# The weight sums of a block product, kept in DRAM, and a ring of nine operand slots in a one-core hybrid decoder layer

## The chip, the cores and the metric

One core of one Trainium2 chip runs the whole layer. The metric is the device time of one execution in microseconds (us). Five engines work side by side and meet at semaphores: TensorE (PE), VectorE (DVE), ScalarE (ACT), GpSimd (POOL) and SyncE (SP). SP issues the plain transfers, and POOL issues those that add to their destination, besides the stores. In the trace they form two queues, q1 (hardware_dynamic, SP) and q0 (software_dynamic, POOL), which share the core's 16 DMA engines.

## What is computed

The layer takes x (512 tokens by 2048) and gives x plus a merge of two token mixers (reference, cut):

```
h = rms_norm(x, norm_w)
proj = h @ w_in                       # q|k|v|z of both branches, beta, alpha, gates
oa = gated_delta_rule(...)  -> rms_norm -> * silu(gdn_z)      # 8 heads of 128
ob = moba_attention(...)             -> * silu(moba_z)        # 8 heads of 128
y_gdn  = oa @ w_out_gdn               # (512 x 1024) @ (1024 x 2048)
y_moba = ob @ w_out_moba              # (512 x 1024) @ (1024 x 2048)
merged = sigmoid(g_gdn) * y_gdn + sigmoid(g_moba) * y_moba
x = x + merged @ w_o                  # (512 x 2048) @ (2048 x 2048)
```

## The kernel before

**Heads.** The first 920 us or so work on the 8 heads. Each head takes eight stripes of w_in (1 MB each, tile `w_raw`, ring of four), and PE's windows of 48 matmuls on a stripe alternate with the small matmuls of the head. Every float32 product is made of three matmuls of rounded parts: ACT writes the high part (`split`, L1328), and DVE the low part (L1784). SP loads stripe n when window n-4 has ended, and ACT splits it when window n-2 has ended. In the last head DVE also makes sums of blocks of h, in 20 steps (`own_step`, L2271, tile `sg`), which POOL stores to DRAM (`store_own`, L757, `row_sums<-sg`). Step (6, 1), the sixth sum of the second half, waits until the store (1, 1) has landed, because it overwrites the tile. SP loads the sums back for the first quad.

**Quads.** Then come ten quads of 1024 output columns: q = 0 to 3 the gates, 4 and 5 y_gdn, 6 and 7 y_moba (Y0 = 4, YB = 6), 8 and 9 the output projection (W0 = 8). Each quad is a 2 by 2 block product made with seven products in place of eight, in the order P11, PS1, PS2, P12, PS4, PS3, P22. Three of the right operands are blocks of the weights as they are (11, 21, 22), and four are sums of blocks: T1 for PS1, T2 for PS2, T3 for PS3, T4 for P22. A product is cut into units of 256 rows by 512 columns of weights (512 KB), four units in quads 0 to 3, 8 and 9 and two in quads 4 to 7. There are 224 units. For unit n ACT writes the high part (`op_hi`, L1627), DVE the low part (`op_lo`, L2285), and PE runs 12 matmuls (L1268, L1270, L1272). ACT may start unit n when PE has ended unit n-4.

**How the sums come about before.** SP loads the blocks into 12 slots of `ops` (A, B, C with four each). DVE forms T1 (`form_t1`, L2386), T2 of the quads with two units (`form_t2`, L2395), T4 (`form_t4`, L2405) and T3 of the gate quads (`form_t3`, L2413) in place, one instruction of 128 x 1024 each. POOL adds a block to a slot by an accumulating DMA (`add_22`, L771; `add_12`, L777). A later load into a slot waits until the sums that read it are formed. DVE's program is a list written out by hand: `forms(q, n)` puts the forming instructions between the `op_lo`.

**Ends of products.** When a product ends, DVE adds its banks to a block (`block_add`, L2305, L2307). In quads 4 to 7 it then multiplies the block by a gate block (L2316), which SP loads (L615, `operands<-gates`) into one of two tiles. In quads 4 and 5 POOL stores the block (`branch_a`, L788). In quads 6 and 7 POOL adds that stored block to it (L794, `e_block<-branch_a`), PE transposes it (`merged_turn`, L1286, four units after the product), ACT copies it, and DVE and ACT make the left operands of quads 8 and 9 (`merged_step` L2258, `merged_hi` L1715, `merged_lo` L2321).

**POOL in a head,** in program order: `decay_parts` (L707 to L718), the load of decay rows (L702), the store of the previous head's attention output (L733, `branch_outputs<-probs`), the cosine products of k and q (L747), the store of o (L749). After the last head come the last store of probs (L766) and the four `add_22` of quad 0. ACT's rounding of the third block sum of quad 0 (L1701) waits for that store of probs, since it writes where probs lay.

## Time and profile before

| what | us |
|---|---|
| median of 3 runs (1563.8 to 1564.4) | 1563.98 |
| the profiled execution | 1563.22 |
| its span, first to last instruction | 1561.6 |
| PE busy in the span | 1532.2 |
| DVE busy | 1108.2 |
| ACT busy | 766.5 |
| POOL busy | 199.0 |

The profiled execution spent 1.6 us outside the span, and it was 0.8 us shorter than the median. PE's clock was granted in full in all of the 40 slices. Idle time of an engine that is not waited for costs nothing, so the reader looks first at where PE stands still, and then at what it stands still for.

### The profile page before, as it was taken

What the parts mean: (1) busy time and instruction counts of PE and PEld (TensorE: products, weight loads), DVE (VectorE), ACT (ScalarE), POOL (GpSimd) and SP (SyncE); (2) the same over time, 40 slices, a digit from 0 to 9 for tenths busy, and PEclk for the clock granted to TensorE, in tenths of its full rate; (3) what the DMA queues carried; (4) which work ended last, traced back from release to release, by engine and by line L of the source; (5) the groups of instructions that cost most, each with busy time, mean ns of one, the idle gap of its engine ahead of it and who ended that gap; (6) DMA issues with size and microseconds to landing.
All of it is one profiled execution on the core that took longest, in us unless ns stands there. A gap on an engine that the chain in (4) does not pass through costs nothing. (4 is left out here: it accounts for less than half of the span.)

```text
span 1561.6 us, 20373 instructions
## 1 busy us (share of the span) xinstructions
PE 1532.2 (98%) x7591; PEld 1280.8 (82%) x7591; DVE 1108.2 (71%) x1371; ACT 766.5 (49%) x1007; POOL 199.0 (13%) x181
## 2 busy tenths in 40 slices
PE   6999999999999999999999999999999999998999
PEld 5888888888888888888888887888888877876787
DVE  6665756756757656557668869867777999878864
ACT  6434435345435345344344347647465865555542
POOL 4202002002002011011020101001010111102020
PEclk9999999999999999999999999999999999999999
DMA  8314315133324233233144357586567688978883
GB/s 274 82 42 128 82 44 145 54 87 102 80 64 124 60 83 98 60 98 111 34 114 108 115 197 207 191 224 215 146 188 196 216 256 242 243 215 167 225 186 56
DMA packets 198047, 217.02 MB, mean 139 GB/s; under 512 B 7843, under 2 KB 140198, under 8 KB 196902
## 3 DMA queue, kind: packets, MB, share of 16 engines
q1 hardware_dynamic: 177030, 162.73, 35.2%
q0 software_dynamic: 20960, 53.52, 14.7%
q8 instruction: 37, 0.61, 0.2%
q14 instruction: 20, 0.16, 0.0%
HBM read 191.03 MB, written 29.39 MB: 141 GB/s over the span
## 5 line engine op out<-in xcount | busy, mean ns | idle before, releaser
L827 PE MATMUL bank<-h_hi_r,w_hi 128*128 128x512 f32 x1008 | 407.4, 404 | 0.0
L831 PE MATMUL bank<-h_hi_r,w_raw_r 128*128 128x512 f32 x1008 | 394.5, 391 | 0.0
L829 PE MATMUL bank<-h_lo_r,w_hi 128*128 128x512 f32 x1008 | 393.6, 390 | 0.0
L2285 DVE TENSOR_TENSOR ring_lo<-operands,ring_hi 128x1024 fp32r<-128x1024 f32 x224 | 271.8, 1223 | 111.0 <-ACT ring_hi L1627 109.4
L1627 ACT ACTIVATE ring_hi<-operands 128x1024 fp32r<-128x1024 f32 x224 | 235.6, 1061 | 213.1 <-PE bank L1272 153.8
L831 PEld LDWEIGHTS bank<-h_hi_r,w_raw_r 128*128 128x128 f32 x1008 | 189.2, 188 | 41.5
L829 PEld LDWEIGHTS bank<-h_lo_r,w_hi 128*128 128x128 f32 x1008 | 189.9, 188 | 34.6
L827 PEld LDWEIGHTS bank<-h_hi_r,w_hi 128*128 128x128 f32 x1008 | 189.9, 188 | 34.0
L1268 PE MATMUL bank<-ring_hi,h_hi_r 128*128 128x512 f32 x480 | 188.9, 393 | 1.8 <-issue 1.4
L1270 PE MATMUL bank<-ring_lo,h_hi_r 128*128 128x512 f32 x480 | 186.8, 389 | 0.0
L1784 DVE TENSOR_TENSOR w_raw_r<-w_raw,w_hi 128x2048 fp32r<-128x2048 f32 x64 | 151.3, 2364 | 32.1 <-ACT w_hi L1328 31.0
L1272 PE MATMUL bank<-ring_hi,h_lo_r 128*128 128x512 f32 x416 | 161.9, 389 | 0.0
L1272 PE MATMUL bank<-ring_hi,sums_r 128*128 128x512 f32 x384 | 149.5, 389 | 0.0
L1268 PE MATMUL bank<-ring_hi,sums_r 128*128 128x512 f32 x320 | 125.5, 392 | 4.3 <-DVE ring_lo L2285 3.1
L1270 PE MATMUL bank<-ring_lo,sums_r 128*128 128x512 f32 x320 | 124.6, 389 | 0.0
L1328 ACT ACTIVATE w_hi<-w_raw 128x2048 fp32r<-128x2048 f32 x64 | 122.1, 1908 | 0.0
L1268 PEld LDWEIGHTS bank<-ring_hi,h_hi_r 128*128 128x128 f32 x480 | 90.1, 188 | 22.0 <-issue 2.0
L1270 PEld LDWEIGHTS bank<-ring_lo,h_hi_r 128*128 128x128 f32 x480 | 90.2, 188 | 18.7 <-issue 0.2
L1272 PEld LDWEIGHTS bank<-ring_hi,h_lo_r 128*128 128x128 f32 x416 | 78.1, 188 | 16.2
L1272 PEld LDWEIGHTS bank<-ring_hi,sums_r 128*128 128x128 f32 x384 | 72.1, 188 | 15.1
L1268 PEld LDWEIGHTS bank<-ring_hi,sums_r 128*128 128x128 f32 x320 | 60.1, 188 | 18.7 <-DVE ring_lo L2285 3.1
L1270 PEld LDWEIGHTS bank<-ring_lo,sums_r 128*128 128x128 f32 x320 | 60.1, 188 | 12.2
(324 smaller groups left out, 2134.9 us busy)
## 6 DMA issues: line engine op xcount, KB each, us to landing
w_raw<-in_w_in_dram SPq DMA_DIRECT2D x64, 1024.0 KB, 6.1
operands<-in_w_in_dram SPq DMA_DIRECT2D x64, 512.0 KB, 4.8
operands<-in_w_o_dram SPq DMA_DIRECT2D x32, 512.0 KB, 5.1
operands<-in_w_in_dram POOLq DMA_DIRECT2D x16, 512.0 KB, 7.8
gates<-e_block POOLq DMA_DIRECT2D x16, 512.0 KB, 5.9
operands<-in_w_out_gdn_dram SPq DMA_DIRECT2D x16, 512.0 KB, 5.4
operands<-gates SPq DMA_DIRECT2D x16, 512.0 KB, 6.6
operands<-in_w_out_moba_dram SPq DMA_DIRECT2D x16, 512.0 KB, 5.8
```

The costliest lines, as they stand in the source:

```text
L827: pe.matmul(PJ[slot % 2][:], w_hi[slot % 2][:, c], h_hi[:, k, :], start=(k == 0), stop=False, skip_group_check=True)
L829: pe.matmul(PJ[slot % 2][:], w_hi[slot % 2][:, c], h_lo[:, k, :], start=False, stop=False, skip_group_check=True)
L831: mm = pe.matmul(PJ[slot % 2][:], w_lo[slot][:, c], h_hi[:, k, :], start=False, stop=(k == KT - 1), skip_group_check=True)
L1268: pe.matmul(ps[:], a_hi, ring_hi[:, n % RINGS, c], start=(FRESH[p] and k == 0), stop=False, skip_group_check=True)
L1270: pe.matmul(ps[:], a_hi, ring_lo[:, n % RINGS, c], start=False, stop=False, skip_group_check=True)
L1272: mm = pe.matmul(ps[:], a_lo, ring_hi[:, n % RINGS, c], start=False, stop=(k == kn - 1), skip_group_check=True)
L1328: act.activation(w_hi[slot % 2][:], raw[slot][:], ACT.Copy).then_inc(s["hi_ready"], 1)
L1627: act.activation(ring_hi[:, n % RINGS, :], operand(q, p, j), ACT.Copy).then_inc(s["op_hi"], 1)
L1784: dve.tensor_tensor(w_lo[slot][:], raw[slot][:], w_hi[slot % 2][:].bitcast(F32), ALU.subtract)\
L2285: dve.tensor_tensor(ring_lo[:, n % RINGS, :], operand(q, p, j), ring_hi[:, n % RINGS, :].bitcast(F32), ALU.subtract).then_inc(s["op_lo"], 1)
```

## The change

The four sums of the blocks of `w_out_gdn`, `w_out_moba` and `w_o` get a home in DRAM (`weight_sums`, 32 MB in all). One eighth of the rows is worked on in each head. SP copies the first addend of T1, T2, T3 and T4 for each of the three weights from DRAM to DRAM between its stripe loads (12 copies a head, 4 MB). POOL adds block 22 to T3 and block 12 to T1 (`sums_13`, six DMAs, 2 MB), then T3 to T2 (`sums_2`, three DMAs, 1 MB), then T2 to T4 (`sums_4`, three DMAs, 1 MB), each a head later than the copies. All are accumulating DMAs with source and destination in DRAM. The last slab's sums are made behind the last head and in quads 0 and 1.

In quads 4 to 9 every unit is then loaded whole, in the order of use, through a ring of nine slots. Unit n may be loaded when `op_lo` of unit n-9 is done. The 40 forming instructions of DVE in those quads (24 in quads 4 to 7, 16 in quads 8 and 9) and the 24 adding DMAs of POOL (16 `add_12`, 8 `add_22`) go. The loads of weights in those quads become 112 where there were 64. Gate loads take fixed places in the stream, 13 units behind the end of the product whose gate tile they reuse. Quads 0 to 3 stay as they are.

```diff
+STREAM = ((SLOT_A, 0), (SLOT_A, 1), (SLOT_A, 2), (SLOT_A, 3), (SLOT_B, 0), (SLOT_B, 1), (SLOT_B, 2), (SLOT_C, 0),
+          (SLOT_C, 1))
...
+T1, T2, T3, T4 = range(4)
+T_FIRST = ((0, 0), (0, 0), (0, 1), (1, 0))
+T_OF = {PS1: T1, PS2: T2, PS3: T3, P22: T4}
+NT_COPIES = 12
...
+        def weight_sum(q, t, j):
+
+            of, at = (2, q - W0) if q >= W0 else ((q - Y0) // 2, q % 2)
+            return t_dram[of][t, UK * j * P:UK * (j + 1) * P, at, :].rearrange("(k p) c -> p k c", p=P)
...
+        def slab(of, t, i):
+
+            r = t_dram[of].shape[1] // H
+            return t_dram[of][t, bass.ds(i * r, r), :, :]
...
+        def block_slab(of, kb, cb, i):
+
+            r = t_dram[of].shape[1] // H
+            return w_blocks[of][kb, bass.ds(i * r, r), :, cb, :]
+
+        residual = ops[:, SLOT_C, 2, :].rearrange("p (t c) -> p t c", t=2)
...
         def source(q, p, j):
 
-            if p == PS4 and ku(q) == 2:
-                return SLOT_A, 2 + j
+            if q >= Y0:
+                return STREAM[streamed(unit(q, p, j))[1]]
...
+                    sp.dma_start(slab(of, t, i), block_slab(of, *T_FIRST[t], i)).then_inc(s["wt_copied"], 16)
+
             def head_loads(i):
+                sp.wait_ge(s["wt_copied"], 16 * NT_COPIES * i)
                 for w, (_, col) in enumerate(STRIPES):
...
                         slot_free(i * NW + w)
                     load(i * NW + w, w % RING, w_in3[:, :, bass.ds(i * P + col, P)])
+                    sum_copies(i, w)
 
             load(0, 0, w_in3[:, :, STRIPES[0][1]:STRIPES[0][1] + P])
...
+            def load_streamed(n):
+
+                q, p, j = place(n)
+                i = n - unit(Y0)
+                slot, u = source(q, p, j)
+                if i < NSTREAM:
+                    before = (PS4, PS3, P22)[slot]
+                    sp.wait_ge(s["op_lo"], unit(Y0 - 1, before, u) + 1)
+                    if slot == SLOT_A:
+                        sp.wait_ge(s["t_formed"], t3_formed(Y0 - 1, u))
+                else:
+                    sp.wait_ge(s["op_lo"], n - NSTREAM + 1)
+                src = weight_sum(q, T_OF[p], j) if p in T_OF else \
+                    right(q, {P11: 0, P12: 1, PS4: 1}[p], {P11: 0, P12: 0, PS4: 1}[p], j)
+                sp.dma_start(ops[:, slot, u, :].rearrange("p (k c) -> p k c", k=UK), src)\
+                    .then_inc(op_loaded[slot][u], 16)
 
...
+            def stream():
+
+                gate_after = {}
+                for b in range(2, 4 * (W0 - Y0)):
+                    q, i = Y0 + (b - 2) // 4, (b - 2) % 4
+                    gate_after[ended(q, BLOCK_PRODUCT[i]) + LEAD + NSTREAM] = (Y0 + b // 4, b % 4)
+                sp.wait_ge(s["wt_13"], 16 * 6 * H)
+                sp.wait_ge(s["wt_2"], 16 * 3 * H)
+                sp.wait_ge(s["wt_4"], 16 * 3 * H)
+                for n in range(unit(Y0), N_UNITS):
+                    if n == unit(Y0) + NSTREAM - 2:
+                        sp.wait_ge(s["pe_unit"], ended(Y0 - 1, PS4))
+                        sp.wait_ge(s["ob_out"], 16 * H)
+                        sp.dma_start(stage(1), o_dram[H:].rearrange("k p t -> p k t")).then_inc(s["stage_b"], 16)
+                    load_streamed(n)
+                    if n == unit(Y0) + NSTREAM - 1:
+                        load_gate(Y0, 0)
+                        load_gate(Y0, 1)
+                    if n in gate_after:
+                        load_gate(*gate_after[n])
...
+            def sums_13(i, done):
+
+                pool.wait_ge(s["wt_copied"], 16 * NT_COPIES * done)
+                for of in range(3):
+                    pool.dma_start(slab(of, T3, i), block_slab(of, 1, 1, i), accum_op=ALU.add).then_inc(s["wt_13"], 16)
+                for of in range(3):
+                    pool.dma_start(slab(of, T1, i), block_slab(of, 0, 1, i), accum_op=ALU.add).then_inc(s["wt_13"], 16)
+
+            def sums_2(i, done):
+
+                pool.wait_ge(s["wt_13"], 16 * 6 * done)
+                for of in range(3):
+                    pool.dma_start(slab(of, T2, i), slab(of, T3, i), accum_op=ALU.add,
+                                   max_dma_last_dim=4 * 2 * COLS).then_inc(s["wt_2"], 16)
+
+            def sums_4(i, done):
+
+                pool.wait_ge(s["wt_2"], 16 * 3 * done)
+                for of in range(3):
+                    pool.dma_start(slab(of, T4, i), slab(of, T2, i), accum_op=ALU.add,
+                                   max_dma_last_dim=4 * 2 * COLS).then_inc(s["wt_4"], 16)
...
                     pool.wait_ge(s["ob"], h)
                     pool.dma_start(o_dram[bass.ds(p + H, 1)].rearrange("o p t -> p (o t)"), pr1[:])\
                         .then_inc(s["ob_out"], 16)
+                    sums_13(p, h)
 
                 if h is last:
                     store_own(1, 1)
@@ -745,8 +810,12 @@
                     pool.wait_ge(s["b_n"], 2 * h + c + 1)
                     pool.wait_ge(s["s_mm"], 4 * h)
                     pool.tensor_tensor(r[:], pt[:, c, :], cos, ALU.mult).then_inc(s["b_cos"], 1)
+                    if c == 0 and p is not None:
+                        sums_2(p, h)
                 pool.wait_ge(s["o_2"], h + 1)
                 pool.dma_start(o_dram[bass.ds(h, 1)].rearrange("o p t -> p (o t)"), o1[:]).then_inc(s["o_out"], 16)
+                if p is not None:
+                    sums_4(p, h)
 
...
+            sums_13(last, H)
             pool.wait_ge(s["ob"], H)
             pool.dma_start(o_dram[2 * H - 1], pr1[:]).then_inc(s["ob_out"], 16)
...
-            def add_12(q, j):
-
-                pool.wait_ge(s["t_formed"], t1_formed(q, j))
-                pool.dma_start(ops[:, SLOT_B, j, :].rearrange("p (k c) -> p k c", k=UK), right(q, 1, 1, j),
-                               accum_op=ALU.add).then_inc(t3_acc[j], 16)
...
             for q in range(NQ):
-                if ku(q) == 4:
+                if q < Y0:
                     add_22(q, 0)
                     add_22(q, 1)
-                if ku(q) == 2:
-                    add_12(q, 0)
-                    add_12(q, 1)
                 if q > 0:
                     finish_block(q - 1, 3)
-                if ku(q) == 4:
+                if q < Y0:
                     add_22(q, 2)
                     add_22(q, 3)
-                if q >= W0:
-                    for j in range(4):
-                        add_12(q, j)
+                if q == 0:
+                    sums_2(last, H)
+                if q == 1:
+                    sums_4(last, H)
                 for i in range(3):
...
-                if p == P11 or p == P12 or (p == PS4 and ku(q) == 2):
-                    act.wait_ge(op_loaded[slot][u], op_loads(q, u, slot))
+                if q >= Y0:
+                    act.wait_ge(op_loaded[slot][u], stream_loads(n))
...
-                elif at < 2:
-                    form_t1(q, at)
-                elif at < 4:
-                    form_t2(q, at - 2)
-                elif 6 <= at < 8:
-                    form_t4(q, at - 6)
```

The order of instructions shows three places. The first is POOL in the last head and behind it. Here `row_sums<-sg` is `store_own`, `weight_sums` the new sums, `branch_outputs` the stores of probs and o, and the last row the adds of quad 0. Before:

```order
L757 DMA row_sums<-sg 128x1024 x3
L733 DMA branch_outputs<-probs 128x512
L757 DMA row_sums<-sg 128x1024 x3
L747 TENSOR_TENSOR k_rope<-pt,cossin 128x512
L757 DMA row_sums<-sg 128x1024 x2
L747 TENSOR_TENSOR q_rope<-pt,cossin 128x512
L749 DMA branch_outputs<-work 128x512
L766 DMA branch_outputs<-probs 128x512
L771 DMA operands<-in_w_in_dram 128x2x512 x4
```

And of the change, first from the probs store of the last head to the three stores behind it, and then from the store of o on:

```order
L797 DMA branch_outputs<-probs 128x512
L766 DMA weight_sums<-in_w_out_gdn_dram 128x512
L766 DMA weight_sums<-in_w_out_moba_dram 128x512
L766 DMA weight_sums<-in_w_o_dram 256x512
L768 DMA weight_sums<-in_w_out_gdn_dram 128x512
L768 DMA weight_sums<-in_w_out_moba_dram 128x512
L768 DMA weight_sums<-in_w_o_dram 256x512
L826 DMA row_sums<-sg 128x1024 x3
```

```order
L816 DMA branch_outputs<-work 128x512
L781 DMA weight_sums<-weight_sums 64x1024 x2
L781 DMA weight_sums<-weight_sums 128x1024
L766 DMA weight_sums<-in_w_out_gdn_dram 128x512
L766 DMA weight_sums<-in_w_out_moba_dram 128x512
L766 DMA weight_sums<-in_w_o_dram 256x512
L768 DMA weight_sums<-in_w_out_gdn_dram 128x512
L768 DMA weight_sums<-in_w_out_moba_dram 128x512
L768 DMA weight_sums<-in_w_o_dram 256x512
L836 DMA branch_outputs<-probs 128x512
L841 DMA operands<-in_w_in_dram 128x2x512 x4
```

The stores (1, 1), (2, 0) and (2, 1) of the block sums now stand behind six adding DMAs, and the last probs store and the adds of quad 0 behind nine.

The second place is DVE at the start of quad 8, with `ring_lo` the `op_lo`, `operands<-operands` the forming of T1, `h_hi`, `sums_r` and `h_lo` the left operands. Before:

```order
L2258 TENSOR_TENSOR h_hi<-h_lo 128x4x256
L2285 TENSOR_TENSOR ring_lo<-operands,ring_hi 128x1024 x2
L2321 TENSOR_TENSOR sums_r<-h_hi,sums_r 128x2048
L2285 TENSOR_TENSOR ring_lo<-operands,ring_hi 128x1024
L2386 TENSOR_TENSOR operands<-operands 128x1024
L2307 TENSOR_TENSOR e_block<-bank,e_block 128x512 x2
L2316 TENSOR_TENSOR e_block<-e_block,operands 128x1024
L2285 TENSOR_TENSOR ring_lo<-operands,ring_hi 128x1024
L2386 TENSOR_TENSOR operands<-operands 128x1024
L2258 TENSOR_TENSOR h_hi<-h_hi,h_lo 128x8x256
L2285 TENSOR_TENSOR ring_lo<-operands,ring_hi 128x1024
```

And of the change:

```order
L2318 TENSOR_TENSOR h_hi<-h_lo 128x4x256
L2345 TENSOR_TENSOR ring_lo<-operands,ring_hi 128x1024 x2
L2381 TENSOR_TENSOR sums_r<-h_hi,sums_r 128x2048
L2345 TENSOR_TENSOR ring_lo<-operands,ring_hi 128x1024
L2367 TENSOR_TENSOR e_block<-bank,e_block 128x512 x2
L2376 TENSOR_TENSOR e_block<-e_block,operands 128x1024
L2345 TENSOR_TENSOR ring_lo<-operands,ring_hi 128x1024
L2318 TENSOR_TENSOR h_hi<-h_hi,h_lo 128x8x256
L2345 TENSOR_TENSOR ring_lo<-operands,ring_hi 128x1024
```

The two forming instructions between them are gone, and the rest keeps its order.

The third place is SP in quad 5, with its loads of weights and of gate blocks (`operands<-gates`). Before:

```order
L551 DMA operands<-in_w_out_moba_dram 128x2x512 x6
L615 DMA operands<-gates 128x1024 x2
L551 DMA operands<-in_w_out_moba_dram 128x2x512 x2
L615 DMA operands<-gates 128x1024 x2
```

And of the change, about one quad of the stream:

```order
L640 DMA operands<-in_w_out_moba_dram 128x2x512 x2
L640 DMA operands<-weight_sums 128x2x512 x4
L640 DMA operands<-in_w_out_moba_dram 128x2x512 x2
L652 DMA operands<-gates 128x1024
L640 DMA operands<-in_w_out_moba_dram 128x2x512 x2
L652 DMA operands<-gates 128x1024
L640 DMA operands<-weight_sums 128x2x512 x2
L652 DMA operands<-gates 128x1024
L640 DMA operands<-weight_sums 128x2x512 x2
```

A quad of 14 units has 14 weight loads where it had 8, and the gate blocks stand singly among them.

## Rows read from the trace of the kernel before

**Rows 1.** The page, busy time of the engines (us, share of the span, instructions).

```profile
PE 1532.2 (98%) x7591; PEld 1280.8 (82%) x7591; DVE 1108.2 (71%) x1371; ACT 766.5 (49%) x1007; POOL 199.0 (13%) x181
```

**Rows 2.** The waits of PE from 1240 to 1460 us.

```profile
PE bank L1268 <- DVE ring_lo L2285: 5.9, 5, 1.5
PE bank L1268 <- ACT operands L1668: 1.8, 2, 1.2
PE bank L1268 <- issue: 1.4, 1, 1.4
PE bank L1286 <- DMA e_block<-branch_a: 0.5, 1, 0.5
```

**Rows 3.** The timeline of PE at one of these stalls.

```profile
1416.02 0.39 PE L1272 MATMUL bank<-ring_hi,sums_r 128*128 128x512 f32 x1
1417.85 0.50 PE L1268 MATMUL bank<-ring_hi,sums_r 128*128 128x512 f32 x1 [1.44 <-DVE ring_lo L2285]
```

**Rows 4.** The timeline of DVE ahead of it.

```profile
1413.24 1.22 DVE L2386 TENSOR_TENSOR operands<-operands 128x1024 f32<-128x1024 f32 x1
```

**Rows 5.** Stretches: busy times of the engines, PEclk, DMA share, GB/s.

```profile
400.00:511.00 111.00, 111.00 (x583) 93.77 (x583) 70.15 (x106) 48.04 (x71) 12.15 (x9) 1.00 0.31 85
1014.00:1030.00 16.00, 16.00 (x73) 13.24 (x72) 6.64 (x6) 8.15 (x11) 3.89 (x4) 1.00 0.84 164
1058.00:1070.00 12.00, 12.00 (x54) 9.94 (x54) 6.93 (x8) 8.08 (x8) 1.16 (x2) 1.00 1.04 393
1529.00:1537.00 8.00, 8.00 (x37) 6.64 (x36) 3.68 (x3) 3.03 (x4) 1.20 (x1) 1.00 0.48 68
917.00:942.00 25.00, 25.00 (x115) 20.13 (x114) 17.57 (x33) 13.42 (x23) 0.23 (x1) 1.00 0.69 260
1255.00:1405.00 150.00, 146.18 (x666) 119.80 (x665) 135.02 (x131) 80.68 (x98) 17.65 (x21) 1.00 0.84 243
```

**Rows 6.** DMA issues of the page (count, KB, us to landing).

```profile
w_raw<-in_w_in_dram SPq DMA_DIRECT2D x64, 1024.0 KB, 6.1
row_sums<-sg POOLq DMA_DIRECT2D x8, 512.0 KB, 5.3
```

**Rows 7.** The timeline of SP and ACT in a head: a stripe's load, and later splits.

```profile
478.18 0.37 SPq L520 DMA_DIRECT2D w_raw<-in_w_in_dram  x1
500.31 1.91 ACT L1328 ACTIVATE w_hi<-w_raw 128x2048 fp32r<-128x2048 f32 x1
```

**Rows 8.** The timeline of POOL, DVE and PE in the last head.

```profile
868.38 0.55 POOL L733 DMA_DIRECT2D branch_outputs<-probs  x1 [4.65 <-DVE probs L2020]
871.24 0.53 POOL L757 DMA_DIRECT2D row_sums<-sg  x1 [2.32 <-DVE sg L2271]
880.51 1.22 DVE L2271 TENSOR_TENSOR sg<-sg,h_hi_r 128x1024 f32<-128x1024 f32 x1
884.11 0.42 DVE L1917 TENSOR_TENSOR inv_a<-bank,inv_a 64x256 f32<-64x256 f32 x1 [1.12 <-PE bank L941]
886.05 0.39 PE L962 MATMUL bank<-v_beta,inv_a 128*128 128x128 f32 x2
```

**Rows 9.** The timeline of POOL, ACT and PE in quad 0.

```profile
947.96 0.54 POOL L766 DMA_DIRECT2D branch_outputs<-probs  x1 [30.73 <-DVE probs L2020]
950.88 1.90 ACT L1701 ACTIVATE sums_r<-sums 128x2048 fp32r<-128x2048 f32 x1
954.77 1.06 ACT L1627 ACTIVATE ring_hi<-operands 128x1024 fp32r<-128x1024 f32 x1 [2.00 <-DMA operands<-in_w_in_dram]
968.89 0.50 PE L1268 MATMUL bank<-ring_hi,sums_r 128*128 128x512 f32 x1 [0.30 <-DVE ring_lo L2285]
```

**Rows 10.** The timeline of DVE, POOL and PE at a merged block.

```profile
1394.94 1.23 DVE L2316 TENSOR_TENSOR e_block<-e_block,operands 128x1024 f32<-128x1024 f32 x1 [3.86 <-DMA operands<-gates]
1396.46 0.84 POOL L794 DMA_DIRECT2D e_block<-branch_a  x1 [8.56 <-DVE e_block L2316]
1404.32 0.87 PE L1286 MATMUL bank<-ident,e_block 128*128 128x128 f32 x6 [0.54 <-DMA e_block<-branch_a]
```

More of the change, by code:

```diff
@@ L84, in t_base, with t4_formed, op_loads, streamed @@
 def t_base(q):
-    return sum(((3 if ku(b) == 4 else 4) - (b >= Y0)) * ku(b) for b in range(q))
+    return 3 * sum(ku(b) for b in range(min(q, Y0)))
 def t1_formed(q, j):
     return t_base(q) + j + 1
-def t2_formed(q, j):
+def t4_formed(q, j):
     return t_base(q) + ku(q) + j + 1
-def t4_formed(q, j):
-    return t_base(q) + (1 if ku(q) == 4 else 2) * ku(q) + j + 1
 def t3_formed(q, j):
-    return t_base(q) + (2 if ku(q) == 4 else 3) * ku(q) + j + 1
-def t3_added(q, j):
-    return 16 * sum(j < ku(b) for b in range(Y0, q + 1))
+    return t_base(q) + 2 * ku(q) + j + 1
 def added(q):
-    return 16 * (sum(ku(b) == 4 for b in range(q)) + 1)
-def op_loads(q, j, slot, nth=0):
+    return 16 * (q + 1)
+def op_loads(q, slot, nth=0):
     before = (1, N1 // RING, 1)[slot]
-    if slot == SLOT_A:
-        return 16 * (before + sum(2 if ku(b) == 4 else 1 for b in range(q)) + nth + 1)
-    return 16 * (before + sum(j < ku(b) for b in range(q)) + 1)
+    return 16 * (before + (2 * q + nth if slot == SLOT_A else q) + 1)
+STREAM = ((SLOT_A, 0), (SLOT_A, 1), (SLOT_A, 2), (SLOT_A, 3), (SLOT_B, 0), (SLOT_B, 1), (SLOT_B, 2), (SLOT_C, 0),
+          (SLOT_C, 1))
+NSTREAM = len(STREAM)
+def streamed(n):
+    return divmod(n - unit(Y0), NSTREAM)
+def stream_loads(n):
+    m, i = streamed(n)
+    return op_loads(Y0, STREAM[i][0]) + 16 * m
 def e_index(q, role):
@@ L227, in hybrid_layer @@
     own_dram = nc.dram_tensor("row_sums", (4, P, 8, HALF), F32, kind="Internal").ap()
+    t_dram = [nc.dram_tensor(f"weight_sums{i}", (4, rows, 2, COLS), F32, kind="Internal").ap()
+              for i, rows in enumerate((D // 4, D // 4, D // 2))]
+    w_blocks = [w[0].rearrange("(b r) (q s c) -> b r q s c", b=2, q=2, s=2) for w in (w_out_gdn, w_out_moba, w_o)]
     m_dram = nc.dram_tensor("branch_a", (2, 4, P, 2 * COLS), F32, kind="Internal").ap()
@@ L521, in load, with sum_copies @@
                     .then_inc(loaded[slot], 16)
+            def sum_copies(i, w):
+                for c in range(w, NT_COPIES, NW):
+                    of, t = c % 3, c // 3
+                    sp.dma_start(slab(of, t, i), block_slab(of, *T_FIRST[t], i)).then_inc(s["wt_copied"], 16)
             def head_loads(i):
+                sp.wait_ge(s["wt_copied"], 16 * NT_COPIES * i)
                 for w, (_, col) in enumerate(STRIPES):
@@ L546, in _ @@
                 load(w, w % RING, w_in3[:, :, STRIPES[w][1]:STRIPES[w][1] + P])
+                for c in range(w - RING, NW, RING):
+                    sum_copies(0, c)
             with sp.Fori(1, H) as i:
@@ L558, in load_11, with load_12 @@
                         sp.wait_ge(s["win_done"], N1 - 3 + j // 2)
-                    elif ku(q - 1) == 4:
+                    else:
                         sp.wait_ge(s["op_lo"], unit(q - 1, PS4, j) + 1)
-                        if q - 1 < Y0:
-                            sp.wait_ge(s["t_formed"], t3_formed(q - 1, j))
-                    elif j < 2:
-                        sp.wait_ge(s["op_lo"], unit(q - 1, PS2, j) + 1)
-                        sp.wait_ge(s["t_formed"], t4_formed(q - 1, j))
-                    else:
-                        sp.wait_ge(s["op_lo"], unit(q - 1, PS4, j - 2) + 1)
+                        sp.wait_ge(s["t_formed"], t3_formed(q - 1, j))
                     load_op(q, SLOT_A, j, 0, 0, j)
-            def load_12(q, units):
-                for j in units:
+            def load_12(q):
+                for j in range(ku(q)):
                     if q == 0:
                         sp.wait_ge(s["win_done"], N1 - 1 + j // 2)
-                    elif j < ku(q - 1):
+                    else:
                         sp.wait_ge(s["op_lo"], unit(q - 1, PS3, j) + 1)
-                    elif j == 3:
-                        sp.wait_ge(s["yT_mm"], 4 + 1)
                     load_op(q, SLOT_B, j, 0, 1, j)
@@ L653, in _ @@
             load_21(0)
-            load_12(0, range(4))
+            load_12(0)
             sp.wait_ge(s["o_out"], 16 * H)
@@ L662, in _ @@
             load_own(3, region(h_lo32, 0, 1), s["rows_loaded"])
-            for q in range(NQ):
+            for q in range(Y0):
                 quad_loads(q)
-            sp.wait_ge(s["op_lo"], unit(LAST, PS4, 0) + 1)
+            stream()
             sp.dma_start(residual, token_block(xs, LAST, 3)).then_inc(s["stage_b"], 16)
```

87 lines of the change are left out of this document (23 added, 64 removed).

## The prediction, as it was made before the result was known

> **What bounds the kernel now.** I read first the page's busy times [rows 1]: PE is busy for 1532.2 of the 1561.6 us of the span, so whatever the change does to other engines counts only where PE stands still for it. Next I read the waits of PE, stretch by stretch. In a head there is none (111.00 of 111 us busy from 400 to 511 us [rows 5]). From 1240 to 1460 us, in quads 4 to 8, there are nine [rows 2]: six for DVE's low part or for a left operand that DVE writes (the row that says "issue" is one of these), two for ACT's copy of a bank, one for a stored branch block. They sum to 9.6 us. PE's timeline says what one costs in full [rows 3]: the matmul after the stall starts 1.83 us after the one before it, where the pitch is 0.23, so 1.60 us is lost and 1.44 of it is listed. With 0.16 us more for each of nine, 11.0 us is what this part of the kernel can give, and no more. Behind 1460 us PE does not wait at all.
>
> DVE is what is late there. In the 1.2 us ahead of the last low part it forms T1 [rows 4], and such a forming instruction stands between low parts in all of these quads. In the stretch from 1255 to 1405 us DVE is busy for 135 of 150 us [rows 5].
>
> **Removed.** In quads 4 to 9 go 40 forming instructions, 1.22 us each [rows 4], started some 1.14 apart: 6.8 us of DVE in a quad of 14 units (38 us of PE), and 9.1 us in quad 8. ACT's high parts no longer wait for them either. That is more than any of the nine stalls, which have at least two forming instructions ahead of them. Without them the left operands of quad 8 (L2258, L1715, L2321) are ready 2 to 4 us earlier too. I count all nine stalls as ended: 11.0 us gained (0 if DVE were only as late for other reasons, and 11.0 is the ceiling).
>
> **DMA work, priced from stretches.** [rows 5] From 1058 to 1070 us plain loads move 393 GB/s at share 1.04: 1.4 us of all engines for 512 KB. From 1014 to 1030 us four adds into SBUF and one store take 0.84 x 16 = 13.4 us, so an add takes 3.0 us. From 1529 to 1537 us one add into DRAM takes 0.48 x 8 = 3.8 us. The new sums read and write DRAM, and the trace has no such add; I bound it by 3.0 and 3.8.
>
> **Added in the heads.** A head gets 4 MB of copies (8 x 1.4 = 11 us) and 4 MB of sums (8 x 3.0 to 3.8 = 24 to 30 us) beside a share of 0.31 over 111 us (34 us): 69 to 75 of 111. A stripe lands in 6.1 us [rows 6] and is first read 22.1 us after its issue [rows 7]; even if it landed twice as slowly behind a copy it would be in time. POOL has 12 more issues of 0.55 to 1.2 us, about 10 us, and is busy for 12 of 111 us. I cost heads 1 to 6 at nothing; what hides them is the ring of four stripes, and if that cover were gone each us would cost PE a us.
>
> **The last head is different.** There POOL issues the probs store at 868.38 and the block store (1, 1) at 871.24, and DVE's step (6, 1) at 880.51 needs that store landed [rows 8]. It lands in 5.3 us [rows 6], so it has 4 us to spare. Now six sums (2 MB) stand in front of it on POOL's queue. If the queue takes them in turn, they last 4 x 3.0 = 12 to 4 x 3.8 = 15.2 us from 868.9, and the store lands 5.3 us later: 886.2 to 889.4. Behind step (6, 1) on DVE stand step (7, 1) and the inverse's last step (884.11), together 2.8 us, and PE's matmul on it stood at 886.05. So PE loses the landing time less 883.2: 3.0 to 6.2 us. A stripe's load in between could add 2; if the store could overtake the sums, it would land at 873.5 + 5.3 = 878.8 and cost nothing. Range 0 to 8; I take 4.0, inside the computed pair and towards its lower end, since issue and completion of the sums overlap.
>
> A rule that bears on this: the Trainium skill ("DMA: Bandwidth & Descriptors", section on queues, rings and completion order, and that on SWDGE, HWDGE and iDMA) says that DMAs issued by GpSimd have one queue, and that an engine takes a ring's descriptors in order. By that rule the store cannot overtake, and the term is 3.0 to 6.2. The same page (anatomy of one DMA) fits a DMA's time as 2.0 us plus its bytes over 436 GB/s; by that the six sums would be over in some 7 us, the store would land by about 880, nothing would be lost here, and the sum would come out at 1556.5. The trace disagrees for adding DMAs: 3.0 us where that rate gives 1.2.
>
> **Quad 0.** From 917 us on POOL puts 3 MB of sums (18 to 23 us) in front of the last probs store and the adds of quad 0, beside 0.69 x 25 = 17 us of other traffic [rows 5]. That is 35 to 40 us of work from 917, so it ends between 952 and 957 if the engines do no more than their nominal share, and near 948 at the 1.1 or so that they sometimes show. The probs store stood at 947.96 and releases ACT's L1701 (950.88); the first add releases the high part at 954.77 [rows 9]. Behind that wait on ACT stand the high parts of all later units. PE started unit 15 at 968.89 after a stall of 0.30, so unit 12 started near 960.3, and its low part was done near 957.4: 2.9 us to spare. A delay of 0 to 8 us costs 0 to 5; I take 1.5. The last 2 MB of sums, in quads 0 and 1, stand behind the adds, and nothing there waits for them.
>
> **The stream.** A quad of 14 units gets 6 more plain loads and 2 fewer adds: 6 x 1.4 - 2 x 3.0 = +2.4 us of DMA work in 38, and the share of 0.84 becomes 0.90 [rows 5]. Quads 8 and 9 get 12 more loads and 8 fewer adds: -7.2 us each. A unit's load is issued nine units (24 us) ahead. So transfers do not become the bound. What can be late is the gate block: its load is issued two units after the product that frees the tile, where before it followed the multiplication at once, and for the third and fourth block of a quad the next product ends two units later. DVE waited 3.86 us for one such block already, and from its multiplication the block went over POOL to a transposition that PE reached 0.54 us early [rows 10]. Three blocks (two of quad 6, one of quad 7) have this chain. I give back 0.7 us on each: 2.0 (0 to 6).
>
> **Sum.** Against the profiled execution (1563.22: span 1561.6 and 1.6 around it): -11.0 + 4.0 + 1.5 + 2.0 = -3.5, 1559.7. The median of before is 0.8 above that execution, so 1560.5.
>
> **Rivals.**
> - *Nothing is given back.* The sums overlap with idle engines, and the store is in time. For it: DMA share 0.31 in the heads. Against: 12 us at least for 2 MB in turn. Time 1553 to 1557. Chance 0.14.
> - *The gain is eaten up.* The store lands at 890 or later and quad 0 costs its 5, or merged blocks cost 2 us each: 1561 to 1567. For it: each of the three terms is bounded by more than I took. Chance 0.28.
> - *Slower, by the last head.* An add between two places in DRAM costs more than either row. At 5.7 us for 512 KB (one and a half times the dearer row) the store (1, 1) lands at 868.9 + 22.8 + 5.3 = 897, PE loses 13.8, and quad 0 costs 5: 1564 - 11 + 2 + 13.8 + 5 = 1574. It decides from about 4.9 us for 512 KB on, where the store lands at 893.8 and the loss there alone is 10.6. For it: the one add into DRAM is dearer than those into SBUF. Chance 0.18.
> - The forecast itself, 1557 to 1561: chance 0.40.
>
> **How the numbers follow.** A measurement of this kernel tells a change from none from about 0.2% (3.1 us) on. Faster is the forecast and the first rival, 0.54; same is the second, 0.28; slower the third, 0.18. The range leaves out the lowest part of the first rival and more than half of the third: 1554 to 1570.
>
> **What would show it.** Right: no stall of PE on `ring_lo` from 1240 us on; PE's waits in the last head near 886 us, on the inverse, with `sg` (L2271 of before) waiting for a DMA of `row_sums`; ACT's wait for adds in quad 0 longer than 2.0. The heads' stretches stay full for PE, with a DMA share near 0.65. Wrong: stalls on stripes in each head, PE waiting for streamed loads in quads 4 to 7, or DMA shares near 1 over a whole quad.

## The result, and the profile after

The changed kernel takes 1578.26 us (median of 4 runs, 1577.59 to 1578.59) against 1564.19 for the kernel before (1563.8 to 1564.61): ratio 1.0089, 95% interval 1.0072 to 1.0107. It is slower by 14 us, where 3.5 us less was forecast, and outside the range.

First the page of the changed kernel: busy times, where [rows 1] stood before.

```profile
span 1576.7 us, 20949 instructions
PE 1537.8 (98%) x7591; PEld 1287.1 (82%) x7591; DVE 1064.6 (68%) x1331; ACT 766.9 (49%) x1007; POOL 251.0 (16%) x253
```

DVE lost 44 us, as it should. PE is busy for 5.6 us more with the same 7591 instructions: some of them run at another clock. The stretches, with the columns of [rows 5], and PE's waits from 1240 to 1460 us ([rows 2] before):

```profile
400.00:511.00 111.00, 111.00 (x582) 93.77 (x581) 70.14 (x107) 48.02 (x71) 22.28 (x21) 1.00 0.63 161
917.00:942.00 25.00, 25.00 (x114) 20.50 (x113) 17.41 (x30) 12.86 (x22) 10.22 (x11) 1.00 0.76 174
1255.00:1405.00 150.00, 144.81 (x648) 119.52 (x648) 112.37 (x110) 84.99 (x102) 9.11 (x14) 0.99 0.81 268
```
```profile
PE bank L1330 <- DVE ring_lo L2345: 5.3, 3, 3.2
PE bank L1330 <- issue: 0.2, 1, 0.2
```

The head is as forecast: PE is full and the DMA share is 0.63. Of the nine stalls none is left, but three others have come, the longest 3.2 us. To see where time goes I put the start of each window and of each unit of PE beside that of the kernel before. The difference grows or shrinks only in these places (us; it begins at +0.4, which is there from the first stripes on):

| place | difference goes from, to | listed waits of PE there |
|---|---|---|
| heads 0 to 6, to window 61 of 64 | +0.4 to +0.4 | none |
| end of head 7 | +0.4 to +8.6 | 6.12 |
| quad 0, units 6 to 17 | +8.6 to +18.6 | 7.17 |
| quad 5, units 125 to 127 | +17.2 to +22.1 | 3.20 |
| quad 6, units 132 to 142 | +21.2 to +23.4 | 2.00 |
| quads 0 to 8, where stalls of before are gone | together -11.6 | |
| unit 184, and to the end | +14.1 | |

**The last head.** Timeline of POOL, DVE and PE of the changed kernel, where [rows 8] stood before:

```profile
869.28 0.91 POOL L766 DMA_DIRECT2D weight_sums<-in_w_out_gdn_dram  x1
...
872.56 2.53 POOL L826 DMA_DIRECT2D row_sums<-sg  x1
...
889.77 1.23 DVE L2331 TENSOR_TENSOR sg<-sg,h_hi_r 128x1024 f32<-128x1024 f32 x1 [8.80 <-DMA row_sums<-sg]
...
892.72 0.76 PE L1024 MATMUL bank<-v_beta,inv_a 128*128 128x128 f32 x2 [6.12 <-DVE inv_a L1977]
...
893.71 0.63 PE L891 MATMUL bank<-h_lo_r,w_hi 128*128 128x512 f32 x1
894.14 0.63 PE L893 MATMUL bank<-h_hi_r,w_raw_r 128*128 128x512 f32 x1
...
898.08 0.39 PE L891 MATMUL bank<-h_lo_r,w_hi 128*128 128x512 f32 x1
898.31 0.40 PE L893 MATMUL bank<-h_hi_r,w_raw_r 128*128 128x512 f32 x1
```

The store waits behind the sums and DVE's step (6, 1) comes 9.3 us late. The view of DMAs for 872.50 to 872.60 us gives the landing of the last sum (issued at 872.00) and of the store (issued at 872.56):

```profile
weight_sums<-in_w_o_dram POOLq DMA_DIRECT2D x1, 512.0 KB, 16.1
row_sums<-sg POOLq DMA_DIRECT2D x1, 512.0 KB, 17.2
```

So the last sum landed at 888.1 and the store at 889.7, where the store took 4.9 us before. Then read the start times: from 893.71 to 894.14 is 0.43 us for one matmul, from 898.08 to 898.31 the usual 0.23. For some 4 us after the stall PE ran at the lower of its two clock levels (1.2 GHz), and lost 2 us more. The stretches of PE alone show it too (PE busy, granted clock, DMA share, GB/s); in the same stretches of the kernel before the clock is 1.00.

```profile
850.00:900.00 50.00, 43.88 (x245) 0.93 0.59 159
900.00:950.00 50.00, 50.00 (x237) 1.00 0.79 188
950.00:1000.00 50.00, 42.34 (x175) 0.93 0.88 254
1250.00:1300.00 50.00, 46.80 (x200) 0.97 0.77 250
```

**Quad 0.** Timelines of SP, ACT and PE of the changed kernel, where [rows 9] stood before:

```profile
937.04 8.01 SPq L692 DMA_DIRECT2D sums<-row_sums  x3
...
957.96 1.91 ACT L1761 ACTIVATE sums_r<-sums 128x2048 fp32r<-128x2048 f32 x1 [9.18 <-DMA sums<-row_sums]
959.78 0.58 ACT L1529 ACTIVATE pt<-bank 128x512 f32<-128x512 f32 x1
...
960.41 4.64 PE L1085 MATMUL bank<-pt,vT 128*128 128x512 f32 x8 [7.17 <-ACT pt L1529]
```

SP loads the row sums back. How long the three loads of `sums<-row_sums` took to land, before and now:

```profile
DMA to landing us min/median/max: 4.8/7.3/9.8
DMA to landing us min/median/max: 16.2/18.3/20.9
```

The longest is in both kernels that of the first, which stands on SP's queue behind six weight loads: it was issued at 937.04 and landed at 957.9. The six took 9.6 to 21.3 us (3.9 to 8.0 before). ACT waits 9.18 us for this first load, in front of a copy of the probabilities that PE needs. What PE waits for is neither the probs store nor an add of quad 0, but a load on another queue.

**Gates.** Timeline of SP, DVE and PE in quad 5:

```profile
1281.22 1.23 DVE L2376 TENSOR_TENSOR e_block<-e_block,operands 128x1024 f32<-128x1024 f32 x1
...
1284.08 0.63 SPq L652 DMA_DIRECT2D operands<-gates  x1
...
1290.58 1.23 DVE L2376 TENSOR_TENSOR e_block<-e_block,operands 128x1024 f32<-128x1024 f32 x1 [3.62 <-DMA operands<-gates]
...
1293.08 0.77 PE L1330 MATMUL bank<-ring_hi,h_hi_r 128*128 128x512 f32 x1 [3.20 <-DVE ring_lo L2345]
1293.64 0.63 PE L1332 MATMUL bank<-ring_lo,h_hi_r 128*128 128x512 f32 x1
```

The tile was free at 1282.45, its next load went out at 1284.08 and landed 6.4 us later; DVE stood 3.62 us at the multiplication with the low parts behind it. Over the kernel DVE now waits 14.6 us for gates in 5 places (3.86 in one before [rows 10]).

### The profile page after: what moved, and what is told of

It reads as the page before. It is cut to its first block, busy times and chain, and to the rows that moved or that the text cites. A ratio compares the mean times of both kernels' runs of the same rounds, so it can differ in the third digit from the quotient of the medians.

```text
span 1576.7 us, 20949 instructions
## 1 busy us (share of the span) xinstructions
PE 1537.8 (98%) x7591; PEld 1287.1 (82%) x7591; DVE 1064.6 (68%) x1331; ACT 766.9 (49%) x1007; POOL 251.0 (16%) x253
## 4 chain that ended last, share of the span: by engine, by line
PE 86%; DMA 6%; DVE 4%; issue 2%; ACT 1%; SPq 1%; POOL 0%; DVEq 0%; ACTq 0%
PE bank L889 14%; PE bank L893 14%; PE bank L891 14%; PE bank L1330 10%; PE bank L1334 10%; PE bank L1332 10%; PE bank L918 2%; DMA operands<-gates 1%; PE bank L991 1%; PE bank L1008 1%; DMA sums<-row_sums 1%; DMA operands<-in_w_in_dram 1%; PE bank L1085 1%; DMA row_sums<-sg 1%; DVE ring_lo L2345 1%
## 5 line engine op out<-in xcount | busy, mean ns | idle before, releaser
L1334 PEld LDWEIGHTS bank<-ring_hi,h_lo_r 128*128 128x128 f32 x416 | 78.1, 188 | 16.2
L1334 PEld LDWEIGHTS bank<-ring_hi,sums_r 128*128 128x128 f32 x384 | 72.1, 188 | 15.1
L1330 PEld LDWEIGHTS bank<-ring_hi,sums_r 128*128 128x128 f32 x320 | 60.1, 188 | 16.4 <-issue 2.9
```

Of the source, the lines that this page charges most:

```text
L1330: pe.matmul(ps[:], a_hi, ring_hi[:, n % RINGS, c], start=(FRESH[p] and k == 0), stop=False, skip_group_check=True)
L1334: mm = pe.matmul(ps[:], a_lo, ring_hi[:, n % RINGS, c], start=False, stop=(k == kn - 1), skip_group_check=True)
```

## The experiments

Each ran on the same chip as the kernel before, which took 1563.96 us (median) beside the first four, 1563.48 beside the next four and 1564.32 beside the last. The changed kernel was not run again beside them, so a difference to its 1578.26 us can be off by some tenths of a us. "Offset" is the difference of PE's start times to the kernel before, as in the table.

**The last head alone.** The six sums of head 6 go behind the stores of the last head (in the table's terms, nothing in front of the store):

```
                 if p is not None:
...
-                    sums_13(p, h)
+                    if h is not last:
+                        sums_13(p, h)
                 if h is last:
                     store_own(1, 1)
                     store_own(2, 0)
                     store_own(2, 1)
+                    sums_13(p, h)
```
`sums_2` of head 6 follows the last store of the head, `sums_4` goes into quad 0.

> Head 6's six first sums are issued behind the row sums' stores of the last head and not ahead of the one at 872.56; its next three behind the heads' last store, and three that stood before quad 0 go into quad 0. All work is done. Theory A (the six sums hold up the store in the same queue, step (6,1) on VectorE comes late, PE waits 6.1 us and then runs some us at the lower clock): the step comes back to within a microsecond of its time of before (880.5), PE's wait at the end of head 7 falls from 6.1 to under 1 us, the offset of PE at unit 0 falls from +8.6 to +0.5 to +1.5; time 1570 to 1571, if quad 0 costs what it did. Theory B (the queue that slows the store is SP's: its 12 copies and the weights' loads use the same DMA engines all along): the store still lands in over 10 us, the wait stays at 4 to 6 us; time 1577 to 1578.

1571.52 us (1570.52 to 1573.52, ratio 1.0053, 1.0037 to 1.0070), 6.7 less than the changed kernel. DVE's wait on `row_sums` is gone, so is the 6.12, and the offset at unit 0 is -0.4, with which this run began. Theory A. Quad 0 costs 11.4 in place of 10.0: 7.9 up to unit 7, and 3.5 at units 15 to 17, where six sums now stand behind the adds in place of three (that these six cause it was not tested by itself).

**Quad 0 alone.** `sums_4` of head 6 and `sums_13` of head 7 go from the stretch ahead of quad 0 to behind its four adds:

```
+                if q == 0:
+                    sums_4(last - 1, last)
+                    sums_13(last, H)
-                if q == 0:
+                if q == 1:
                     sums_2(last, H)
-                if q == 1:
+                if q == 2:
                     sums_4(last, H)
```

> The last three sums of head 6 and the first six of head 7 (4.5 MB) go out of the stretch ahead of quad 0 into quad 0, the later ones a quad later each. All work is done. Theory A (those sums share the DMA engines with the loads of the row sums on SP's queue; the first lands in 16 us in place of 5, ScalarE waits for it ahead of the copy that PE waits for, and PE loses 7.2 us and some at the lower clock): the load lands in 5 to 7 us, PE's wait of 7.2 us at unit 6 is gone, the offset between unit 0 and unit 17 falls from +10.0 to under +1; time 1568 to 1569. Theory B (the prediction's: the probs store and quad 0's adds in GpSimd's queue are what is late): here they stand ahead of all those sums too, so the same total; but then the waits that go are those of VectorE and ScalarE for the accumulated operands and not that for the row sums. Theory C (quad 0 is limited by its own 8 MB and not by the sums): no change, 1577 to 1578.

These are nine sums of 3 MB in all (the 4.5 MB of the expectation is too much). 1570.11 us (1569.49 to 1573.71, ratio 1.0048, 1.0031 to 1.0065). The first load of the row sums lands in 9.9 us, where it took 20.9 in the changed kernel and 9.8 before; the 16 and 5 of the expectation are the shortest of the three loads, and ACT waited for the first. Timeline of ACT of this kernel, for the two ACT rows above:

```profile
948.32 1.91 ACT L1763 ACTIVATE sums_r<-sums 128x2048 fp32r<-128x2048 f32 x1
950.18 0.60 ACT L1531 ACTIVATE pt<-bank 128x512 f32<-128x512 f32 x1
```

Theory A: no wait is listed at either, and PE's 7.17 is gone. The offset at unit 14 is +8.7 (+8.2 at unit 0). But from unit 14 to 19 it grows to +12.8: the four loads that ACT then waits for 2.1 to 3.0 us each land in 10.4 to 11.5 us (3.6 to 5.6 before), beside the sums. So from unit 0 to 17 the offset grows by 2.3, where under 1 was expected, and up to unit 20 quad 0 costs 4.7 in place of 10.0. The time is 8.2 us less, where 9.3 to 10.3 were expected, and 2.0 of the 8.2 come from quad 5, where the stall was 2.58 us in place of 3.20 and no lower clock followed it.

**Both.** All 24 sums of heads 6 and 7 (8 MB) go behind the adds of quads 0 (12), 1 (6) and 2 (6). The 12 MB of the expectation is too much.

> All 24 sums of heads 6 and 7 are issued in quads 0 to 2 (12, 6 and 6), behind the four adds of each. All work is done. Theory A (the two stalls of 6.1 and 7.2 us with what follows each at the lower clock are the whole cost ahead of quad 4): offset of PE at unit 17 under +1.5; what is left is the gain of the nine stalls (-11.3) and the gates' loss (+6.8); time 1560 to 1561. Theory B (the 12 MB moved into quads 0 to 2 delay the adds there, PS2 units wait): up to +4 us in quads 1 to 3, 1562 to 1565.

1562.29 us (10 runs, 1560.6 to 1563.52, ratio 0.9988, 0.9978 to 0.9997): 16 us less than the changed kernel, and within 0.2% of the kernel before. From the start to unit 15 the offset grows by 0.4, so the two stalls are gone as theory A says. Units 15 to 19 cost 2.7, and the time lies in the range of theory B and not in that of A: both hold in part. At the gates the offset grows by 6.7.

**Gates sooner.** With the third, and

```
-                    gate_after[ended(q, BLOCK_PRODUCT[i]) + LEAD + NSTREAM] = (Y0 + b // 4, b % 4)
+                    gate_after[ended(q, BLOCK_PRODUCT[i]) + LEAD + NSTREAM - 1] = (Y0 + b // 4, b % 4)
```

> As the third, and each gate's load stands one unit sooner in SP's stream: it is let go at the split of the unit at which the block that frees its buffer is gated, and no longer one unit later. Theory A (the place of the load in the stream makes the gates late: 14.6 us of VectorE's waits, PE loses 4.8 at quad 5 and 2.2 at quad 6): VectorE's wait for the gates falls under 5 us, PE loses under 1 us at units 126 and 140; time 1553 to 1555. Theory B (a gate is late because its 1 MB lands in 6.9 us beside two units' loads, wherever it stands): the waits move, the time stays at 1560 to 1561. Theory C (SP now waits at the gate and issues the next streamed units late): PE waits for operands at quads 5 and 6, 1560 or above.

1555.25 us (1554.8 to 1555.38, ratio 0.9945, 0.9928 to 0.9961), 7.0 less than the third. The waits of DVE of this kernel, the row for gates:

```profile
DVE e_block L2381 <- DMA operands<-gates: 0.8, 1, 0.8
```

Theory A. The gates' loads take longer here (median 7.6 us to landing, 6.9 in the changed kernel), so it is their place that counted.

**Spread.** With the fourth; the sums of `sums_13` behind the gate block 1 of quad 0 and the adds of quad 1, the rest behind gate block 1 of quad 1 and the adds of quad 2.

```
-                if q == 0:
-                    sums_13(last - 1, last)
-                    sums_13(last, H)
                 if q == 1:
-                    sums_2(last - 1, H)
-                    sums_2(last, H)
+                    sums_13(last, H)
...
                 for i in range(3):
                     finish_block(q, i)
+                    if (q, i) == (0, 1):
+                        sums_13(last - 1, last)
+                    if (q, i) == (1, 1):
+                        sums_2(last - 1, H)
+                        sums_2(last, H)
```

> As the fourth, with the 24 sums of heads 6 and 7 spread: none ahead of the second third of quad 0, then six there (behind the store of the gate block 1), six behind the adds of quad 1, six behind the store of its gate block 1, six behind the adds of quad 2. All work is done. Theory A (in the fourth kernel 12 sums in a row slow the loads of quad 0's PS4 units to 10 us, ACT waits four times some 2.8 us for them and PE loses 2.7 us at units 15 to 19): those waits and the loss go, the offset of PE between unit 0 and unit 124 falls from +2.2 to under +0.7; time 1552 to 1553. Theory B (the loss comes with the amount of sums in a stretch of quads and only moves with them, to the loads of quad 1): 1555 as the fourth.

1552.48 us (1551.4 to 1553.13), ratio 0.9925 (0.9909 to 0.9942): theory A, and a version that is faster than both kernels by 11 and 26 us. The offset is 0.0 at unit 0, -0.8 at unit 124 and -11.7 at unit 184. The largest waits of PE of this kernel (the first two are at the start, before the heads; the three that are not shown are of 0.2 each):

```profile
PE bank L1264 <- DVE x_tiles L2249: 11.2, 1, 11.2
PE bank L1264 <- DVE h_lo_r L2255: 2.5, 2, 1.7
PE bank L1336 <- DVE ring_lo L2351: 0.8, 1, 0.8
PE bank L997 <- DVE inv_a L1983: 0.4, 1, 0.4
```

**What an add ahead of the store costs.** Two kernels: the changed one with the six sums as plain copies (without `accum_op`, so this kernel leaves out six of the additions), and the first experiment with the three sums of T3 (1 MB) left ahead of the store.

> The changed kernel with one edit: in the last head the six sums ahead of the row sums' store are plain copies (the same places and sizes, nothing is added), so these slabs are not the sums. Theory A (the six hold up the store because an adding DMA takes two to three times a plain one: 3.0 to 3.8 us for 512 KB against 1.4): four times 1.4 is 5.6 us, the store lands 6 to 9 us after its issue in place of 17, step (6, 1) starts at 880 to 883 in place of 889.8, PE waits under 1 us in place of 6.1 there and the 2 us at the lower clock go too; with quad 0 as it was 1569 to 1571. Theory B (the place in the queue counts and not the kind, six DMAs of any sort take about the same): step (6, 1) at 886 or later, PE waits 3 us or more, 1575 to 1578.

> As the first experiment, but the three sums of T3 (1 MB) stay ahead of the row sums' store and only those of T1 go behind the stores. All work is done. Theory A (the store waits for the bytes ahead of it at 3.0 to 3.8 us for 512 KB and has 4 us to spare): 1 MB takes 6 to 7.6 us, the store lands near 881 to 883, PE loses 0 to 1 us at the end of head 7; time as the first experiment's (1571.5) to 1.5 above. Theory B (what counts is that an adding DMA stands ahead of it at all, with a wait for its completion): PE loses over 3 us there; 1575 or more.

1572.55 us (1571.95 to 1573.85) and 1571.80 (1569.8 to 1575.89). Timelines of DVE and PE, of the kernel with plain copies and then of that with three sums:

```profile
884.38 1.23 DVE L2342 TENSOR_TENSOR sg<-sg,h_hi_r 128x1024 f32<-128x1024 f32 x1 [4.22 <-DMA row_sums<-sg]
887.34 0.46 PE L1035 MATMUL bank<-v_beta,inv_a 128*128 128x128 f32 x2 [1.53 <-DVE inv_a L1988]
```
```profile
883.42 1.23 DVE L2335 TENSOR_TENSOR sg<-sg,h_hi_r 128x1024 f32<-128x1024 f32 x1 [2.89 <-DMA row_sums<-sg]
886.37 0.46 PE L1028 MATMUL bank<-v_beta,inv_a 128*128 128x128 f32 x2 [0.21 <-DVE inv_a L1981]
```

Counted from the probs store ahead of them (868.74, 867.95, 868.30), step (6, 1) starts 21.0 us later with six sums, 16.4 with six copies, 15.1 with three sums. So the last 1 MB of sums takes 5.9 us, 3.0 for 512 KB, and the same step with copies is 4.6 us shorter, 1.15 for each of four times 512 KB: about 1.8 for a copy. The landings inside one kernel lie further apart, since the stripe's load and SP's copy share the engines: 3.3 to 3.4 us for 512 KB of sums in the changed kernel (876.3 for the first, 888.1 for the last), some 2.2 with copies (874.7 to 882.4). Theory A for the three sums. For the copies it holds in kind, but 1.8 is more than my 1.4: the step starts at 884.4 and not by 883, PE waits 1.5 and not under 1, and the time is 1.5 us above the expected. The Trainium skill ("DMA: Bandwidth & Descriptors", queues, rings and completion order) says that a DMA engine takes the descriptors of one ring in order, but that completion need not follow this order. Here both did: in the last head of all three kernels the transfers of POOL's queue landed in the order of issue, and the store never overtook what stood ahead of it.

**The order on ScalarE.** In the changed kernel:

```
-            own_hi(PS1)
             pTc(last, 3)
+            own_hi(PS1)
             copy_out(0, P11)
```

> The changed kernel with two of ScalarE's instructions exchanged: the high part of the loaded row sums (own_hi of PS1) stands behind the last head's copy of the probabilities and no longer ahead of it. All work is done, the sums stay where they are. Theory A (PE's 7.2 us in quad 0 come from this order on ScalarE: the copy is ready long before, and waits behind an instruction that waits for a load of the row sums that lands in 16 us): PE goes on past that copy, and waits next at unit 8, whose left operand is the row sums' and can be ready near 962.3, so 3 to 4 us of the 7.2 come back and some of those at the lower clock; 1573 to 1575. Theory B (the copy, or the probabilities that it reads, is late itself): no change, 1578.

1577.90 us (1576.48 to 1579.71): no gain, and the expected 3 to 4 us are a miss. The copy that PE waited for now starts at 949.78 in place of 959.78, so it was ready long before, as theory A says. But PE's wait only moved to unit 8. Timelines of ACT, DVE and PE of this kernel:

```profile
949.78 0.60 ACT L1529 ACTIVATE pt<-bank 128x512 f32<-128x512 f32 x1 [1.76 <-PE bank L1079]
957.05 1.91 ACT L1761 ACTIVATE sums_r<-sums 128x2048 fp32r<-128x2048 f32 x1 [6.67 <-DMA sums<-row_sums]
...
958.99 2.29 DVE L2381 TENSOR_TENSOR sums_r<-sums,sums_r 128x2048 fp32r<-128x2048 f32 x1 [5.79 <-ACT sums_r L1761]
...
963.47 0.68 DVE L2080 TENSOR_TENSOR probs<-bank,mgt 128x512 f32<-128x512 f32 x1
...
964.25 0.77 PE L1330 MATMUL bank<-ring_hi,sums_r 128*128 128x512 f32 x1 [6.87 <-DVE probs L2080]
```

DVE has an instruction of its own for the late load in its order (`own_lo`), and behind it, after one low part and one forming instruction, the read of a bank that unit 8 writes again. The left operand of unit 8 comes from the same late load, so even without that read it would have been ready only at 961.3. The load was late for two engines, and freeing one of them freed nothing. I had looked at ACT's order alone.

**The clock after a stall.** The fifth kernel with three stalls put in:

```
+AGAIN = {unit(1, P12, 1): 6, unit(2, P12, 1): 8, unit(3, P12, 1): 11}
...
+                for _ in range(AGAIN.get(n, 0)):
+                    act.activation(ring_hi[:, n % RINGS, :], operand(q, p, j), ACT.Copy).then_inc(s["hc_set"], 1)
+                    times[0] += 1
+                    act.wait_ge(s["hc_set"], 2 + NHC + 2 + times[0])
```

> The fifth kernel with three stalls of PE put in on purpose, one each in quads 1, 2 and 3 at the second unit of P12, by ScalarE making the high part of that unit's operand 6, 8 and 11 times more (the same values in the same place). PE stands still for about 1.5, 4 and 7 us. Theory A (PE's own idle time brings the granted clock down to its lower level for some us after it, as behind the 6.1, 7.2 and 3.2 us of the changed kernel, and not behind its 2.0 us): the matmuls behind the two longer stalls have a pitch of 0.43 us for some us, with 1.5 to 2.5 us lost more on each; behind the short one the pitch stays at 0.227 and nothing more is lost. Theory B (the clock fell there because of the adding DMAs and the full DMA engines beside PE): the pitch stays at 0.227 behind all three, since the sums are spread here and the DMA share is lower; the time is that of the fifth kernel and the three stalls alone.

1566.45 us (one run). The stalls came out at 0.94, 2.98 and 6.25 us. Timeline of PE of this kernel after the second:

```profile
1121.55 0.50 PE L1337 MATMUL bank<-ring_hi,h_hi_r 128*128 128x512 f32 x1 [2.98 <-DVE ring_lo L2358]
1121.88 0.39 PE L1339 MATMUL bank<-ring_lo,h_hi_r 128*128 128x512 f32 x1
```

After the third (6.25) the starts are 1204.25, 1204.85, 1205.27, 1205.70 and so on, 0.43 apart to 1208.68 and 0.23 apart from 1209.23 on; the offset grows by 2.3 beyond the stall. After the second it grows by nothing. The stretch of the third stall and that behind it, with the columns of [rows 5] (the granted clock, the DMA share and GB/s stand last):

```profile
1198.00:1204.20 6.20, 0.00 (x1) 0.00 (x0) 1.23 (x2) 6.07 (x7) 0.00 (x0) 0.83 0.00 0
1204.20:1209.00 4.80, 4.75 (x11) 3.76 (x12) 4.80 (x5) 3.50 (x5) 0.00 (x0) 0.51 0.45 116
```

Theory A for the long one: no sum is under way and the DMA share is 0.00, so the clock falls without either. The middle stall came out shorter than meant (3 us and not 4), and it lost nothing more.

## Why the prediction was wrong, step by step

**Nine stalls end, -11.0: right.** -11.6 in the changed kernel and -12.2 in the fifth (from +0.5 at unit 15 to -11.7 at unit 184), a little more than the 11.0 that the text called the ceiling.

**Heads at nothing: right.** No growth of the offset to window 61; share 0.63 where near 0.65 was computed.

**The last head, +4.0: the path right, the size wrong; it measured +8.2.** The store did wait its turn behind the sums. The step that failed is the landing time, "12 to 4 x 3.8 = 15.2 us from 868.9, and the store lands 5.3 us later: 886.2 to 889.4", with the choice of 4.0 "towards its lower end, since issue and completion of the sums overlap". The six sums lasted 19.2 us from 868.9: the first landed only at 876.3, the last at 888.1. The store landed 1.6 us behind them and not 5.3. So there was an overlap, and it was more than eaten up by what the sum left out: SP's stripe load (1 MB, named with "could add 2" and not counted) and SP's 256 KB copy went through the same engines, at a DMA share of 1.08 from 870 to 888 us. They landed in 13.0 and 14.4 us, and in 6.9 and 7.5 in the first experiment, where no sums ran beside them. That SP's transfers are what stretched the sums is argued from this; no run took them away. Two errors of opposite sign put the landing (889.7) just above the computed upper end, so that is in part luck. From the landing on the text is right: 6.1 of the 8.2 is the stall. The other 2.1 is the clock, which no term had.

**Quad 0, +1.5 (0 to 5): wrong in its mechanism; it measured +10.0.** The step "the probs store stood at 947.96 and releases ACT's L1701" followed only the transfers that share POOL's queue with the sums. It priced the work of all engines from 917 on (35 to 40 us, and they were indeed full from 930 to 960), but asked only which POOL transfer ends late. The size of that work was right, with the last of the sums landing at 952.8. What PE waited for was a load on SP's queue, issued at 937.04 into the same engines, which landed in 20.9 us where it took 9.8. The second and third experiments show it: without the sums it lands in 9.9, and the 7.2 us are gone. Of the 10.0, 7.2 is that stall and about 2.3 the clock.

**Gates and merged blocks, +2.0 (0 to 6): the delay right, the place wrong; it measured +7.1.** The text named the later issue of the gate's load, and then priced three merged blocks of quads 6 and 7. No merged block waited. DVE itself waited (3.62, 2.40, 2.41 and two more), and the low parts behind it in its order kept PE: 3.2 and some 1.6 for the clock in quad 5, 2.2 in quad 6. One unit sooner in the stream brought 7.0 back.

**Sum:** -11.6 + 8.2 + 10.0 + 7.1 = +13.7 against -3.5. Even every upper bound (8 + 5 + 6 - 11 = +8) did not reach it: what was missing altogether is the load on SP's queue and the clock after the three long stalls (2.1 + 2.3 + 1.6 = 6.0).

**The third rival** had the sign, and 1574 near the time, for another reason: it needed 4.9 us for an add of 512 KB, and the runs give 3.0 to 3.4 here and 4.0 in quad 0. That its time comes near is luck. The runs measure every term. Open are what share SP's transfers had in the 19.2 us of the last head, why stalls of like length, 2.5 to 3 us, differ (below), and how the engines divide themselves between the two queues.

## What to carry to other kernels

A group of transfers put into a gap can slow every transfer that is issued while it runs, on any queue: list all of them with their first reader, not only those behind it in its own queue. Then ask of each late transfer which instructions wait for it in the order of every engine. Count a stall of PE with the clock behind it: here those from 2.47 us on often cost some 2 us beyond their length. If a change gains where it should and loses elsewhere, the work can often be put at another time: here 24 transfers put off into quads 0 to 2, and 14 gate loads let go one unit sooner, turned +14 us into -11.

## What the runs showed of the hardware

- **The clock after a stall.** After stalls of PE of 3.20, 6.12, 6.25 and 7.17 us matmuls of 512 columns had a pitch of 0.43 us in place of 0.227 for some 3 to 5 us, which cost 1.6 to 2.4 us; so it was after every stall of 3.2 us or more in the eleven traces (behind the start). After stalls of up to 2.2 us none had. In between the length doesn't decide: in quad 5 those of 2.47, 2.52, 2.74 and 2.90 us (experiments seven, three, six and one) brought the pitch of 0.43 and cost some 1.6 us more, that of 2.58 (experiment two) and the 2.98 of the last experiment brought neither. The Trainium skill ("TensorE: Matmul & The Clock Gate", part 1 on the clock gate) has the same mechanism, a gate that passes half of the clock's pulses when PE has been idle. Its section on the back-to-back issue gap gives a spacing of N/1.2 ns for N columns at the lower level, from which 427 ns for 512 columns is an estimate; the traces agree with 0.43 us.
- **DMAs from DRAM to DRAM.** By the differences above 512 KB took 3.0 us as an add and about 1.8 as a copy, one after the other in GpSimd's queue, beside SP's traffic; in quad 0, beside SP's loads, the 3 MB of adds landed 4.0 us apart for each 512 KB (from 930.7 to 952.8).
- **A load beside another queue's adds.** 1 MB into SBUF landed in 16.2 to 20.9 us, where it took 4.8 to 9.8, behind and beside 3 MB of sums that filled the DMA engines (share 1.02 from 926.70 to 952.80 us).
